# Weight sums of three seven-product output stages made ahead in the feed-forward stage and kept in DRAM

## The reference, cut to what matters

```python
h2 = _rms(x, norm2_g)
x = x + (silu(h2 @ w_ffn_gate) * (h2 @ w_ffn_up)) @ w_ffn_down     # "up", then "down": K = 2816
...
u = rmsnorm(h, norm_w[layer])
h = h + concatenate([y_a, y_b], axis=-1) @ even_w_out              # "out2": K = 2048
...
h = h + (rmsnorm(o, norm_w) * silu(g)) @ odd_w_out                 # "out3": K = 2048
return rmsnorm(h, final_norm_w)
```

## Time and profile before

| | |
|---|---|
| median of 3 runs | 4127.33 us (4123.76 to 4135.82) |
| the profiled execution | 4121.29 us, its span 4119.6 us |
| PE, DVE, POOL, ACT busy | 90%, 63%, 37%, 44% of the span |
| up, PE's first to last product | 1012 to 1452 us |
| down, its 77 items | 1455.2 to 1697 us |
| out2, its 56 items | 2725.1 to 2905 us |
| out3, its 56 items | 3922.1 to 4103 us |

### The profile page before, as it was taken

The page is one execution under the profiler, slowest core; times in us unless marked ns, Lnnn a source line. Parts: engine busy times, 40 slices in busy tenths (PEclk is TensorE's granted clock), DMA queues, the critical chain, the costliest instruction groups (busy, mean ns, idle before and its releaser), DMA issues. The chain is left out here.

```text
span 4119.6 us, 53124 instructions
## 1 busy us (share of the span) xinstructions
PE 3725.1 (90%) x19688; PEld 3153.4 (77%) x19688; DVE 2585.7 (63%) x4175; ACT 1830.0 (44%) x3365; POOL 1536.4 (37%) x1346
## 2 busy tenths in 40 slices
PE   7899777799999979999999978879999999999878
PEld 6667656577788858778887766757899999999766
DVE  6569783426444477513576568877566777677576
ACT  3135555415333324521344358843455545555534
POOL 1423220033444452211234451132466666666341
PEclk9969898899999989999999999989999999999889
DMA  4222301363222263521244586943211111111053
GB/s 149 81 78 80 116 14 39 125 210 120 80 84 80 85 235 119 168 83 69 67 128 153 171 182 126 171 174 113 85 42 42 52 37 43 51 42 47 24 201 128
DMA packets 327357, 421.66 MB, mean 102 GB/s; under 512 B 43627, under 2 KB 215180, under 8 KB 326572
## 3 DMA queue, kind: packets, MB, share of 16 engines
q1 hardware_dynamic: 286108, 291.89, 23.1%
q0 software_dynamic: 38688, 122.18, 10.0%
q10 hardware_dynamic: 2304, 4.20, 0.3%
HBM read 302.04 MB, written 116.15 MB: 102 GB/s over the span
## 5 line engine op out<-in xcount | busy, mean ns | idle before, releaser
L119 PE MATMUL hg_acc<-l_first_ws,l_XT 128*128 128x256 f32 x2880 | 359.6, 285 | 0.0
L119 PEld LDWEIGHTS hg_acc<-l_first_ws,l_XT 128*128 128x128 f32 x2880 | 348.8, 192 | 0.0
L119 PE MATMUL hg_acc<-l_XT,hg_ws 128*128 128x512 f32 x1440 | 343.4, 394 | 0.0
L119 PEld LDWEIGHTS hg_acc<-l_XT,hg_ws 128*128 128x128 f32 x1440 | 266.9, 189 | 52.5
L4637 POOL TENSOR_TENSOR hg_DD<-hg_BB 128x256 f32<-128x256 f32 x224 | 174.0, 777 | 260.1 <-PE hg_pA L4396 133.4
L4494 DVE TENSOR_TENSOR hg_DD<-hg_Q,hg_DD 128x256 f32<-128x256 f32 x224 | 204.6, 913 | 73.3 <-ACT hg_DD L4565 73.2
L119 PE MATMUL even_bank<-l_first_ws,l_XT 128*128 128x512 f32 x888 | 206.2, 390 | 3.2 <-PEq L857 1.9
L119 PE MATMUL even_bank<-even_ws,l_XT 128*128 128x512 f32 x876 | 204.4, 390 | 0.0
L119 PEld LDWEIGHTS even_bank<-l_first_ws,l_XT 128*128 128x128 f32 x888 | 166.2, 188 | 40.7 <-issue 6.0
L119 PEld LDWEIGHTS even_bank<-even_ws,l_XT 128*128 128x128 f32 x876 | 163.9, 188 | 33.9
L119 PE MATMUL am_g_acc<-l_XT,am_ws 128*128 128x512 f32 x768 | 179.6, 397 | 8.6 <-ACT am_stage L2082 8.6
(11 more groups left out here) (794 smaller groups left out, 9579.9 us busy)
## 6 DMA issues: line engine op xcount, KB each, us to landing
l_first_raw<-in_odd_w_in SPq DMA_DIRECT2D x62, 512.0 KB, 5.3
l_first_raw<-in_even_w_in SPq DMA_DIRECT2D x16, 1024.0 KB, 5.3
l_room_tiles<-in_w_ffn_down SPq DMA_DIRECT2D x58, 256.0 KB, 5.4
da_first_X<-q_k_hi POOLq DMA_DIRECT2D x24, 512.0 KB, 7.8
da_first_X<-q_k_lo POOLq DMA_DIRECT2D x24, 512.0 KB, 13.3
l_room_tiles<-hidden SPq DMA_DIRECT2D x45, 256.0 KB, 4.7
l_room_tiles<-in_even_w_out SPq DMA_DIRECT2D x42, 256.0 KB, 5.2
l_room_tiles<-y_even SPq DMA_DIRECT2D x37, 256.0 KB, 4.9
```

The source lines that it names most:

```text
L119: mm = pe.matmul(out, lhs(p, k), rhs(q, k), start=start and i == 0, stop=stop and i == n - 1, skip_group_check=skip)
```

## The change

The weight sums of the three output stages are made in `swiglu_up`. Three DRAM arrays (TW) of K/2 rows by 4 x 512 columns take them. For each of the 27 pairs k (11 of down, 8 of out2, 8 of out3; a **block** below) SP loads the four weight tiles as two DMAs of 512 KB into one of two places in `y`, DVE makes the four sums by four instructions (`block_sums`), and SP stores them by one DMA of 1 MB. Blocks fall to chunks 3 to 20, two in chunks 3, 5, ... 19 and one in chunks 4, 6, ... 20: the first right after the first gate's multiplication (P4), the second at the head of the P3 branch, ahead of the second gate's addition.

In `reduce_blocks` the weight operand of every item is loaded as one tile, from W or from TW, into a ring of R = 8 tiles, eight items ahead. All loads of an item (its weight tile, its token tile, early and late token tiles, a piece of the residual) count on one semaphore of eight, in SP's order, and whoever waits for an item's load waits for all of them. The two early token tiles of a k come one k per 1.5 items. The token sums stay on GpSimd, except the last one of each k, which goes to DVE. The residual pieces go from GpSimd's queue to SP's, with items (P1, KP//2), (P6, 0), (P5, 0) and (P7, 0). The load of `pre` goes to SP, its rounding from P3 to P4. GpSimd no longer waits for `after` itself. The diff, cut to its core:

```diff
+MADE = ("P5", "P7", "P4", "P6")
...
+    NS, R = 4, 8
...
+    early_at, late_at, last_at = {}, {}, {}
     for k in range(KP):
-        groups_at.setdefault(min(2 * KP - 1, F0 + 1 + (7 * k) // 4), []).append(k)
-    sums_at = {}
-    for k in range(KP):
-        sums_at.setdefault(min(place["P6", k] - 1, F0 + (7 * k) // 4 + 2), []).append(k)
+        early_at.setdefault(F0 + 2 + (3 * k) // 2, []).append(k)
+        late_at[place["P5", k] + R] = k
+        last_at[place["P3", k] - 3] = k
+    part_at = {place["P1", KP // 2]: (0, 0), place["P6", 0]: (0, 1), place["P5", 0]: (1, 1), place["P7", 0]: (1, 0)}
+    early_of = {k: j for j, some in early_at.items() for k in some}
+    late_of = {k: j for j, k in late_at.items()}
+    part_of = {part: j for j, part in part_at.items()}
+    loads = [0] * N
+    for j in range(F0, N):
+        loads[j] = 1 + (items[j][0] in ("P1", "P2", "P4")) + 2 * len(early_at.get(j, [])) + (j in late_at) + (j in part_at)
...
+        def weights(name, k):
+            if name in ("P1", "P2"):
+                return W[rows(k, name == "P2"), 0:NC]
+            if name == "P3":
+                return W[rows(k, 1), NC:D]
+            q = MADE.index(name)
+            return TW[k * P:(k + 1) * P, q * NC:(q + 1) * NC]
 
...
+            s = (i - F0) % R
+            return {"P1": RA[k], "P2": ring_a[s], "P6": RA[k], "P5": RA2[k], "P7": RA3[k], "P3": RA[k],
+                    "P4": ring_a[s]}[name], ring_w[s]
+
+        def wait_loaded(eng, j):
+
+            eng.wait_ge(item_ld[(j - F0) % R], sum(loads[j % R if j % R >= F0 else j % R + R:j + 1:R]) * DMA)
...
                 sp.wait_ge(begun.split, F0)
-                ahead = range(F0, min(KP, F0 + FIRST))
-                for k in ahead:
-                    sp.dma_start(RB[k], weights(k, 0, 0)).then_inc(first_ld[(k - F0) % FIRST], DMA)
-                sp.dma_start(RB3[0], weights(0, 0, 1)).then_inc(group_ld[0], DMA)
-                sp.dma_start(RB2[0], weights(0, 1, 1)).then_inc(group_ld[0], DMA)
+
+                def load(j, dst, src):
+                    sp.dma_start(dst, src).then_inc(item_ld[(j - F0) % R], DMA)
+
+                for j in range(F0, F0 + R):
+                    load(j, ring_w[j - F0], weights(*items[j]))
                 for stored, value in after:
                     sp.wait_ge(stored, value)
-
-                def ring_free(k, second, first, then):
...
+                whole = res.rearrange("(t p) n -> p t n", p=P)
+                for j in range(F0, N):
+                    name, k = items[j]
+                    if j >= F0 + R:
+                        wait_split(sp, *items[j - R])
+                        load(j, ring_w[(j - F0) % R], weights(name, k))
+                    if name == "P1":
+                        load(j, RA[k], tokens(k, 0, 0))
+                    if name == "P2":
+                        load(j, ring_a[(j - F0) % R], tokens(k, 1, 0))
+                    if name == "P4":
+                        load(j, ring_a[(j - F0) % R], tokens(k, 1, 1))
+                    for q in early_at.get(j, []):
+                        load(j, RA3[q], tokens(q, 0, 1))
+                        load(j, RA2[q], tokens(q, 1, 1))
+                    if j in late_at:
+                        load(j, RA2[late_at[j]], tokens(late_at[j], 1, 0))
+                    if j in part_at:
+                        t, n = part_at[j]
+                        load(j, y[:, t * HT:(t + 1) * HT, n * NC:(n + 1) * NC], whole[:, t * HT:(t + 1) * HT, n * NC:(n + 1) * NC])
+                    if j == place["P7", KP // 2]:
+                        if final:
+                            sp.dma_start(gb[:, :], g.partition_broadcast(P)).then_inc(g_ld, DMA)
+                        else:
+                            sp.dma_start(gc[:, :], g.rearrange("(k p) -> p k", p=P),
+                                         allow_slow_non_contiguous=True).then_inc(g_ld, DMA)
+                    if not final and j == place["P4", 6]:
+                        sp.wait_ge(s4, KP)
+                        pre.load(sp, pre_ld)
...
-                    if not final and name == "P3" and k >= KP - PARTS:
+                    if not final and name == "P4" and k >= KP - PARTS:
...
-                def weight_sums(k):
-                    dve.wait_ge(group_ld[k % GROUP], (k // GROUP + 1) * 4 * DMA)
-                    wait_split(dve, "P1", k)
-                    dve.tensor_tensor(RB[k], RB3[k], RB[k], ALU.subtract).then_inc(t1, 1)
-                    dve.tensor_tensor(RB3[k], RB3[k], RB2[k], ALU.subtract)
-                    dve.wait_ge(t1, k + 1)
-                    dve.tensor_tensor(RB2[k], RB2[k], RB[k], ALU.subtract).then_inc(t2, 1)
-
-                def last_weight_sum(k):
-                    dve.wait_ge(late_ld[k % LATE], (k // LATE + 1) * 2 * DMA)
-                    dve.tensor_tensor(RB2[k], RB[k], RB2[k], ALU.subtract).then_inc(t4, 1)
+                def last_token_sum(k):
+                    wait_loaded(dve, late_of[k])
+                    wait_split(dve, "P6", k)
+                    dve.tensor_tensor(RA[k], RA2[k], RA[k], ALU.subtract).then_inc(s4, 1)
...
-                    for q in sums_at.get(i, []):
-                        weight_sums(q)
-                    if name == "P7":
-                        last_weight_sum(k)
+                    if i in last_at:
+                        last_token_sum(last_at[i])
...
-                def last_token_sum(k):
-                    pool.wait_ge(late_ld[k % LATE], (k // LATE + 1) * 2 * DMA)
-                    pool.tensor_tensor(RA[k], RA2[k], RA[k], ALU.subtract).then_inc(s4, 1)
...
-                for stored, value in after:
-                    pool.wait_ge(stored, value)
-                whole = res.rearrange("(t p) n -> p t n", p=P)
                 for k in range(KP):
-                    if k == 1:
-                        pool.dma_start(y[:, 0:HT, 0:NC], whole[:, 0:HT, 0:NC]).then_inc(res_ld, DMA)
-                    if k == KP - 1:
-                        pool.wait_ge(res_ld, DMA)
-                        pool.dma_start(y[:, 0:HT, NC:D], whole[:, 0:HT, NC:D]).then_inc(res_ld, DMA)
                     token_sums(k)
-                pool.dma_start(y[:, HT:TT, NC:D], whole[:, HT:TT, NC:D]).then_inc(corner_ld, DMA)
-                for k in range(KP):
-                    last_token_sum(k)
-                pool.wait_ge(s4, KP)
-                if not final:
-                    wait_split(pool, "P7", KP - 1)
-                    pre.load(pool, pre_ld)
-                pool.wait_ge(t4, KP)
-                pool.wait_ge(corner_ld, DMA)
-                pool.dma_start(y[:, HT:TT, 0:NC], whole[:, HT:TT, 0:NC]).then_inc(corner_ld, DMA)
...
+        blocks = [(W, TW, k) for W, TW in outputs for k in range(W.shape[0] // P // 2)]
+        room = [X7.y[:, 3 + 2 * s:5 + 2 * s, :].rearrange("p a n -> p (a n)").rearrange("p (a n) -> p a n", a=4) for s in range(2)]
+        blocks_at = {}
+        for b in range(len(blocks)):
+            blocks_at.setdefault(3 + b * (chunks - 4) // len(blocks), []).append(b)
...
+                def load_blocks(b):
+                    W, _, k = blocks[b]
+                    KP = W.shape[0] // P // 2
+                    if b >= 2:
+                        sp.wait_ge(b_st[b % 2], b // 2 * DMA)
+                    for q in range(2):
+                        sp.dma_start(room[b % 2][:, 2 * q:2 * q + 2, :].rearrange("p a n -> p (a n)"),
+                                     W[(q * KP + k) * P:(q * KP + k + 1) * P, :]).then_inc(b_ld[b % 2], DMA)
+
+                def store_sums(b):
+                    _, TW, k = blocks[b]
+                    sp.wait_ge(b_made, 3 * (b + 1))
+                    sp.dma_start(TW[k * P:(k + 1) * P, :], room[b % 2][:, :, :].rearrange("p a n -> p (a n)")).then_inc(b_st[b % 2], DMA)
...
+                    if c == 2:
+                        sp.wait_ge(t3_lo, KH)
+                        sp.wait_ge(t4_lo, KH)
+                        load_blocks(0)
+                        load_blocks(1)
+                    for b in blocks_at.get(c - 2, []):
+                        store_sums(b)
+                        if b + 2 < len(blocks):
+                            load_blocks(b + 2)
+                for b in blocks_at.get(chunks - 2, []) + blocks_at.get(chunks - 1, []):
+                    store_sums(b)
+                    if b + 2 < len(blocks):
+                        load_blocks(b + 2)
...
+                def block_sums(b):
+
+                    b11, b12, b21, b22 = (room[b % 2][:, q, :] for q in range(4))
+                    dve.wait_ge(b_ld[b % 2], (b // 2 + 1) * 2 * DMA)
+                    dve.tensor_tensor(b11, b12, b11, ALU.subtract).then_inc(b_made, 1)
+                    dve.tensor_tensor(b12, b12, b22, ALU.subtract)
+                    dve.wait_ge(b_made, 3 * b + 1)
+                    dve.tensor_tensor(b22, b22, b11, ALU.subtract).then_inc(b_made, 1)
+                    dve.wait_ge(b_made, 3 * b + 2)
```

(8 more changed lines are left out.)

134 lines of the change are left out of this document (27 added, 107 removed).

## The result

The changed kernel takes 4099.69 us in the median of 4 runs (4096.52 to 4103.42), the kernel before beside it on the same chip 4128.49 us (4123.76 to 4135.82). The ratio is 0.9929, 95% interval 0.9911 to 0.9947: faster by 29 us, 0.7%. Predicted were 4093 us and 35 us.

The account below looks back on a forecast made before the run. DVE, colliding with GpSimd in SBUF, was taken to bound the output stages' first parts, PE the rest. 4121.3 - 45.7 (output stages) + 11 (up) = 4086.6, plus 6.0 to the median: 4093 us, range 4062 to 4124 (own 4080 to 4106).

Parts of the forecast that it names:

- What bounds the output stages: First parts of down, out2, out3: PE waits for a full DVE, whose SBUF instructions pair with GpSimd's at 1.70 us.
- The output term: Weight sums leaving DVE start (P6, 0) earlier by 15.7 us in out2, 14.2 in out3, 15.8 in down: 45.7 saved.
- The up term: In up, two blocks delay a chunk's gate additions and `u2`, so PE waits 1.2 us in 9 chunks: 11 us.
- SP's step: In up, SP waits for block stores, so weights land late; put at 0, or 2.5 us per pair of chunks.
- rival D: Late weights in up because SP waits for the stores: 22 us on top of the forecast, 4115; chance 0.12.
- B: Output stages: DVE and GpSimd collide little at the port, PE sets the pace, 70.3 us gained: 4068; chance 0.12.
- C: Output stages: GpSimd shuts DVE out in runs, half of the time; gain 29 us, 4109; chance 0.12.
- E: Slower than before: block sums sit on PE's path in up, all 65 us making 4147; chance 0.09.
- F: No change: loads bind the output stages until (P6, 0), 4127; chance 0.05.
- T: Output stages: DVE and GpSimd take strict turns at 1.85 us a pair; gain 34.1 us, 4104; chance 0.10.
- The sum: Whole kernel: profiled 4121.3 - 45.7 + 11 = 4086.6 us, plus 6.0 to the median, stated as 4093; chance 0.40.
- The signs: Profile: DVE idle 10% or more before out2's (P6, 0), 1.70 us pairs, 1.2 us waits in every second chunk of up.

Follow-up runs that it names:

- e10: Changed kernel with three idle subtractions per k put back on DVE where the weight sums were made before; 4156.05 us, ratio 1.0070 to the kernel before.
- e6: Changed kernel with the three token sums of each k moved from GpSimd to DVE in the output stages; 4074.05 us, ratio 0.9872 to the kernel before.
- e8: Changed kernel with four weight tiles instead of eight ahead of the first tokens and the first residual quarter later; 4083.85 us, ratio 0.9892.
- e2: Kernel before with only the changed kernel's swiglu_up, whose stored sums nobody reads; 4148.25 us, ratio 1.0067.
- e4: Changed kernel with SP's block loads that wait for a store put behind the next chunk's weights in up; 4088.89 us, ratio 0.9919.
- e9: Changed kernel with e8's edits, e6's token sums, e4's load order and the second block summed in the next chunk; 4040.26 us, ratio 0.9789.
- e3: Changed kernel with a chunk's second block moved behind the second gate's addition and the following split; 4095.67 us, ratio 0.9929.

## Why the prediction was right, and where its numbers were off

**What bounds the output stages** held. The gain comes from DVE's instructions beside GpSimd at 1.70 us a pair. The pairs are 1.70 us apart after the change as well; e10 gives the instructions back and loses the time; e6 takes GpSimd away, and the item falls to PE's 2.73 us. The Trainium skill, page "SBUF — State Buffer", section "SBUF: two separate sides", states that a DVE instruction with two SBUF inputs and a GpSimd one exclude each other for a whole instruction. Taken one after the other, 0.60 and 1.25 us would be 1.85 us a pair and the stages 34.1 us shorter, an estimate; the rows give 1.70 and 41.8. The trace agrees that one of each passes per pair in the changed kernel; the price is the measured one. Down's start was carried over as 1470 where the distance used for out2 gives 1470.6, and 2.25 MB was given 7 us where the rate used for the 2 MB gives 7.3: slips of under 1 us, which make the forecast gain too large.

**The output term**, 45.7 us, measured 41.8: down 14.5 for 15.8, out2 13.7 for 15.7, out3 13.6 for 14.2. The step that was off is the start of the sums. The prediction put it 15.4 us after PE's first item in out2 (2740.5 against 2725.1); it was 17.3 (2754.18 against 2736.86), and 15.8 and 16.3 in out3 and down for 15.4 and 14.8: 3.8 us in all. From 2736 to 2749 the queues moved 292 GB/s, not the 320 that it took. From the start of the sums to (P6, 0) it said 41.8, 41.8 and 61.1 us, and 42.0, 42.0 and 61.5 were measured: the pairs are right to 0.4 us in every stage. What it left unasked is which loads stand ahead of the first tokens; e8 gets 15.9 us from that order.

**The up term**, 11 us, measured 18.9 (19.6 in e2). The nine waits of 1.2 us in the chunks with two blocks are there, at 1.12 to 1.13 us each and 10.2 in all, and e4 leaves exactly them: 11.5 us over before. The seven others are 5.6 us, and PE's longer busy time is the rest. What was mis-sized is SP's step, put at 0 with a remark of 2.5 us per pair of chunks at a 1 MB store of 7 us. It priced both 1 MB stores by the 4.7 us of a 512 KB one. The first took 3.9 us, the second, which shares the queues with the loads of the block after next, 8.2, and the weights went out at 1245.12, with SP there 13.8 us after its first store. The 4 us by which ACT could be late for nothing were 5.5, but ACT was late by 5.4 to 7.0. That is rival D at a third of its price, 7.4 us by e4 for its 22. (The sum that ends at 1241.6 should end at 1241.2; nothing hangs on it.) The sentence that none of PE's waits would be ended by a DMA was true to the letter and misled: PE's row names ACT, and the DMA stands one step further back, in ACT's own wait.

**The rivals.** B fell on the 3.40 us items. C fell: the 8.23 us runs are gone with the change in all three stages, which the prediction had not forecast. The traces point at GpSimd's issues of the residual, which the prediction counts among what moves at no cost; no run tried them alone. E fell: PE's wait per block is 18.9 / 27 = 0.7 us, under the 1.7 from which it would have decided. F fell in e6 and e9, where the same queues carry 300 to 353 GB/s. T is told apart by the rows and not by the time: its 4104 is nearer to the measured 4099.7 than the forecast is, but its gain of 34.1 us is 7.7 below the 41.8 of the stages, and its 1.85 us a pair would be seen. That e3 left the nine waits had its reason already written down in the prediction: its working goes through both gates' additions, and the experiment's theory looked at one.

**The sum**: -45.7 + 11 = -34.7 forecast, -41.8 + 18.9 = -22.9 by stages, and -28.8 between the medians. Both terms erred the same way, by 3.9 and 7.9 us, so by the stages the forecast promised 11.8 us too much. The 4093 is 6.7 us below the measured 4099.7, inside the forecast's own range, as is the changed kernel's whole spread; that the medians came out nearer than the stages is luck, the spread between executions and not the working.

**The signs.** (P6, 0) comes 59.3, 57.8 and 77.8 us after PE's first item for the forecast's 57, 57 and 76 (out3 had 71.4 before and not the 73 named there). DVE is idle for 23% of the time from 2740 to (P6, 0) of out2, nearly all of it ahead of the sums; once they run it is as full as before. The waits in up were to stand in every second chunk, nine in all, and stood in 16 chunks.

## What to carry to other kernels

Before work is moved between DVE and GpSimd, ask whether they touch SBUF at the same time: here a pair costs 1.70 us where DVE alone needs 0.60 an instruction, so by the stages the helper engine cost 29 us rather than saving any (e6). In a queue that serves two purposes, put what waits for its own result (a load that waits for a store) behind what others wait for: that and the place of one block made 108 sums, their loads and their stores free. And when two edits act on one start, look at the start as well as at the end of the stage: 3.8 and 6.4 us alone and 15.9 together came from starts that added and a stretch behind them that did not. Last, an experiment that gives work back is not the kernel before: e10 was 17 us slower than it, and 11 of them lay ahead of the work.

## What the runs showed of the hardware that was not expected

- DVE and GpSimd at 128x512 in SBUF: 1.70 us a pair in the three output stages of the changed kernel, with no long lock-out left, while the kernel before has a DVE instruction of 8.2 to 8.3 us in each of the three (out2's in the earlier trace rows) and two more of 4.6. All of them, and the five of e2, start 0.52 to 0.54 us after GpSimd issues a DMA between its sums; that the issue is the cause was not tried.
- The DMA engines kept 353 GB/s at a share of 0.99 for 52 us while PE was busy for 51 of them (e9). The matmuls were no slower for it: the median one started 0.227 us after the one before, as in out3's second part before the change at 99 GB/s.
- Late weights cost PE nothing up to 5.5 us of ACT's wait and everything beyond: in all the kernels of this study that have such waits, PE's wait is ACT's less 5.47 to 5.50 us.
- A 1 MB store landed after 3.9 us in eight of the nine first places (4.5 in one), and after 8.0 to 8.6 us beside 1 MB of loads issued just ahead of it (changed kernel, up); in e4, where the loads come later, all are at 3.8 to 5.2.
